# A third buffer for the samples' caches, and the attention sink as a 257th score column

## The reference, cut to what matters

```
def sink_attention(q, k, v, mask, sink):
    s = einsum(q, k) * HEAD_DIM ** -0.5            # a block of 128 queries against 256 keys
    s = where(mask, s, -inf)
    m = maximum(max(s, axis=-1), sk)               # sk: the sink of the head
    p = exp(s - m)
    p = p / (sum(p, axis=-1) + exp(sk - m))
    return einsum(p, v)
```

```
q = (h @ w_xq_l).reshape(B, L, X_HEADS, X_HEAD_DIM)
s = einsum(q, mk) * X_HEAD_DIM ** -0.5
p = softmax(s); o = einsum(p, mv)
return o @ w_xo_l
```

## Time and profile before

| | before |
|---|---|
| median of 3 runs | 3469.14 us (3467.0 to 3477.67) |
| the profiled execution | 3462.95 us |
| its span, first to last instruction | 3461.2 us |
| mean granted TensorE clock | 0.98 of full speed |
| PE / PEld busy | 3247.4 us (94%) / 3077.2 us (89%) |
| DVE busy | 2324.1 us (67%) |
| ACT busy | 1185.9 us (34%) |
| POOL busy | 679.0 us (20%) |
| DMA | 245.87 MB, mean 71 GB/s |

### The profile page before, as it was taken

The page is one execution under the profiler, slowest core; times in us unless marked ns, Lnnn a source line. Parts: engine busy times, 40 slices in busy tenths (PEclk is TensorE's granted clock), DMA queues, the critical chain, the costliest instruction groups (busy, mean ns, idle before and its releaser), DMA issues. The chain is left out here.

```text
span 3461.2 us, 51914 instructions
## 1 busy us (share of the span) xinstructions
PE 3247.4 (94%) x21872; PEld 3077.2 (89%) x21872; DVE 2324.1 (67%) x3509; ACT 1185.9 (34%) x1849; POOL 679.0 (20%) x274
## 2 busy tenths in 40 slices
PE   7999889899899999999989998898998999999997
PEld 7998769788799999999889987698887999999996
DVE  6776782834467677777787767737345767777776
ACT  5342363434432222212344424533344222222212
POOL 1111131012312212222111111310123221212220
PEclk9999999999899999999999999999999999999998
DMA  5112223213411111111121122332044111111111
GB/s 177 44 44 63 76 80 128 75 43 119 183 50 43 49 43 55 39 54 43 54 82 40 50 68 73 107 111 73 26 158 157 43 50 43 49 43 55 40 57 52
DMA packets 71176, 245.87 MB, mean 71 GB/s; under 512 B 7969, under 2 KB 22561, under 8 KB 65825
## 3 DMA queue, kind: packets, MB, share of 16 engines
q1 hardware_dynamic: 70656, 242.50, 20.7%
q10 hardware_dynamic: 288, 0.06, 0.0%
HBM read 214.20 MB, written 23.04 MB: 69 GB/s over the span
## 5 line engine op out<-in xcount | busy, mean ns | idle before, releaser
L258 PE MATMUL ps<-hh,w_hi 128*128 128x344 f32 (+2 forms) x4320 | 1417.6, 328 | 84.1 <-DVE w_lo L252 26.0
L260 PE MATMUL ps<-hh,w_lo 128*128 128x344 f32 (+2 forms) x4320 | 1391.2, 322 | 0.0
L259 PE MATMUL ps<-hl,w_hi 128*128 128x344 f32 (+2 forms) x4320 | 1391.0, 322 | 0.0
L243 POOL TENSOR_TENSOR w_lo<-w_raw,w_hi 128x1024 fp32r<-128x1024 f32 x270 | 678.8, 2516 | 2719.6 <-ACT w_hi L235 2719.6
L258 PEld LDWEIGHTS ps<-hh,w_hi 128*128 128x128 f32 x4320 | 822.8, 190 | 112.8 <-issue 53.5
L259 PEld LDWEIGHTS ps<-hl,w_hi 128*128 128x128 f32 x4320 | 822.0, 190 | 3.2 <-issue 1.1
L260 PEld LDWEIGHTS ps<-hh,w_lo 128*128 128x128 f32 x4320 | 822.0, 190 | 0.0
L2591 DVE TENSOR_TENSOR Y<-Y,ps 128x344 f32<-128x344 f32 x912 | 433.2, 513 | 155.7 <-PE ps L260 155.7
L235 ACT ACTIVATE w_hi<-w_raw 128x1024 fp32r<-128x1024 f32 x296 | 310.6, 1052 | 440.6 <-PE ps L260 383.8
L2390 ACT ACTIVATE f_c<-f_u,cT 128x1032 f32<-128x1032 f32 (+1 forms) x92 | 111.4, 1213 | 634.6 <-DVE f_u L2556 628.0
L259 PE MATMUL ps<-f_glo,w_hi 128*128 128x344 f32 x960 | 308.0, 321 | 0.0
(11 more groups left out here) (356 smaller groups left out, 3730.0 us busy)
## 6 DMA issues: line engine op xcount, KB each, us to landing
w_raw<-in_w_stream SPq DMA_DIRECT2D x296, 512.0 KB, 3.5
out_y_cols<-xT SPq DMA_DIRECT2D x9, 1376.0 KB, 6.3
xT<-out_y_cols SPq DMA_DIRECT2D x2, 4128.0 KB, 14.0
mem_keys<-in_cache_mem_k SPq DMA_DIRECT2D x8, 1024.0 KB, 5.0
mem_values<-in_cache_mem_k SPq DMA_DIRECT2D x8, 1024.0 KB, 6.3
mem_keys<-in_cache_mem_v SPq DMA_DIRECT2D x8, 1024.0 KB, 5.1
mem_values<-in_cache_mem_v SPq DMA_DIRECT2D x8, 1024.0 KB, 6.9
xT<-in_x_cols SPq DMA_DIRECT2D x3, 1376.0 KB, 12.4
```

Of the source, the lines that this page charges most:

```text
L243: nc.gpsimd.tensor_tensor(w_lo[:, SLOT[m], :], w_raw[:, m % RR, :], w_hi[:, SLOT[m], :].bitcast(F32), ALU.subtract).then_inc(lo_done["pool ...
L258: nc.tensor.matmul(out, whi, mhi, start=start, stop=False)
L259: nc.tensor.matmul(out, whi, mlo, start=False, stop=False)
L260: return nc.tensor.matmul(out, wlo, mhi, start=False, stop=stop)
```

## The change

Two edits that share nothing.

**The caches** get three buffers in turn: the keys' tile, columns 768 to 1023 of the 8 slices of `Y` (8 pieces of 1 KB on each partition), and the values' tile. Transfers 0 and 1 wait for the prompt's last scores, transfer 2 for its last values, transfer t from 3 on for the sample t - 3. In PE's order, one sample moves ahead of each of unit(1, 6) and unit(1, 7).

```
-                    return flat[t % 2]
+                    tiles = (mkT[:], Y[:, :, 768:SEQ], mv_tile[:])
+                    return tiles[t % 3]
...
                     def caches(t):
-                        if t >= 2:
-                            sp.wait_ge(s["s_done"], t - 1)
-                        elif t == 1:
+                        if t >= 3:
+                            sp.wait_ge(s["s_done"], t - 2)
+                        elif t == 2:
                             sp.wait_ge(s["pv"], 32)
                         else:
                             sp.wait_ge(s["scores"], n)
...
                     caches(0)
                     caches(1)
+                    caches(2)
                     load_slabs(sp, first + 2)
-                    for t in range(2, 2 * NS):
+                    for t in range(3, 2 * NS):
                         caches(t)
                         if t in (4, 6, 8):
                             load_slabs(sp, first + t // 2 + 1)
...
-                    sample_values(8)
-                    sample_values(9)
+                    for t in (8, 9, 10):
+                        sample_values(t)
                     unit(1, 6)
-                    sample_values(10)
                     sample_values(11)
+                    sample_values(12)
                     mean(1)
                     unit(1, 7)
-                    for t in (12, 13, 14, 15):
+                    for t in (13, 14, 15):
                         sample_values(t)
```

```
+                SK = 2 * P + 1
+                S = [xT[:, i, 0:4 * SK] for i in (5, 6, 7)]
...
                             for h in range(4):
-                                act_c(nc.scalar.activation(view(S[g % 3], g)[:, h, :], view(S[g % 3], g)[:, h, :], ACT.Exp,
-                                                           bias=st[:, 1, h:h + 1], accum_out=st[:, 3, h:h + 1]))
-                            nc.scalar.activation(st[:, 4, :], st[:, 2, :], ACT.Exp).then_inc(s["exp"], 1)
+                                last = nc.scalar.activation(view(g)[:, h, :], view(g)[:, h, :], ACT.Exp,
+                                                            bias=st[:, 1, h:h + 1], accum_out=st[:, 2, h:h + 1])
+                            last.then_inc(s["exp"], 1)
+                            if g + 3 < n:
+                                act.wait_ge(s["exp"], g + 1)
+                                sink_column(g + 3)
+
+                        def sink_column(g):
+                            sk = sinks[:, l, :].rearrange("p (k a j) -> p a k j", k=NKV, a=2)[:, g % 2]
+                            nc.scalar.activation(sink_view(g), sk, ACT.Copy).then_inc(s["sinks_in"], 1)
...
                             dve.wait_ge(s["scores_used"], g + 1)
+                            dve.wait_ge(s["sinks_in"], g + 1)
...
-                            dve_c(nc.vector.tensor_reduce(st[:, 0, :], sv, AX.X, ALU.max))
-                            dve_c(nc.vector.tensor_tensor(top, top, sk, ALU.max))
-                            dve_c(nc.vector.tensor_tensor(diff, sk, top, ALU.subtract))
+                            dve_c(nc.vector.tensor_reduce(st[:, 0, :], view(g), AX.X, ALU.max))
                             nc.vector.tensor_scalar(st[:, 1, :], st[:, 0, :], -1.0, None, ALU.mult).then_inc(s["negmax"], 1)
...
-                            dve_c(nc.vector.tensor_tensor(st[:, 3, :], st[:, 3, :], st[:, 4, :], ALU.add))
-                            dve_c(nc.vector.reciprocal(st[:, 5, :], st[:, 3, :]))
+                            dve_c(nc.vector.reciprocal(st[:, 3, :], st[:, 2, :]))
```

More of the change, by code:

```diff
@@ L391, in stage_window @@
                 vtok = rs[:, 0:SEQ].rearrange("p (b d) -> p b d", b=NB)
-                S = [xT[:, i, 0:1024] for i in (5, 6, 7)]
+                SK = 2 * P + 1
+                S = [xT[:, i, 0:4 * SK] for i in (5, 6, 7)]
                 PT = [xT[:, i, 0:1024] for i in (0, 1)]
-                small = tmp("win_small", [P, 3, 8, 4])
+                small = tmp("win_small", [P, 3, 4, 4])
                 mh, ml = tmp("mem_hi", [P, KT, NMEM], F32R), tmp("mem_lo", [P, KT, NMEM], F32R)
@@ L397, in stage_window @@
                 s = {n: sem(f"w_{n}") for n in (
-                    "v_turned", "v_copied", "kv_out", "scores", "scores_used", "negmax", "exp", "probs", "turned",
+                    "v_turned", "v_copied", "kv_out", "sinks_in", "scores", "scores_used", "negmax", "exp", "probs", "turned",
                     "turned_copied", "pv", "out_hi", "out_used", "rows_hi", "rows_lo", "mem_in", "m_hi", "m_lo", "m_out", "t_done",
@@ L407, in keys_of, with view, keys_view, sink_view @@
                     return P if g < 2 else 0
-                def view(t, g):
-                    return t.rearrange("p (h k) -> p h k", h=4)[:, :, keys_of(g):]
+                def view(g):
+                    return S[g % 3].rearrange("p (h k) -> p h k", h=4)[:, :, keys_of(g):]
+                def keys_view(g):
+                    return S[g % 3].rearrange("p (h k) -> p h k", h=4)[:, :, keys_of(g):2 * P]
+                def sink_view(g):
+                    return S[g % 3].rearrange("p (k j c) -> p k j c", k=NKV, j=2)[:, :, :, 2 * P]
                 def scores_of(g):
@@ L461, in turn @@
                                     last = nc.tensor.transpose(ps[:, 4 + half, P * h:P * h + P],
-                                                               S[g % 3][:, 256 * h + P * half:256 * h + P * half + P], ident[:])
+                                                               S[g % 3][:, SK * h + P * half:SK * h + P * half + P], ident[:])
                             last.then_inc(s["turned"], 1)
@@ L542, in copy @@
                                                  ps[:, 4 + h0:6, :], ACT.Copy).then_inc(s["turned_copied"], 1)
+                        for g in range(3):
+                            sink_column(g)
                         act.wait_ge(s["v_turned"], 1)
@@ L597, in before @@
                             dve.wait_ge(s["scores_used"], g + 1)
+                            dve.wait_ge(s["sinks_in"], g + 1)
                             st = small[:, g % 3]
-                            sk = sinks[:, l, :].rearrange("p (k a j) -> p a k j", k=NKV, a=2)[:, g % 2]
-                            top, diff = (st[:, i, :].rearrange("p (k j) -> p k j", k=NKV) for i in (0, 2))
-                            dve_c(nc.vector.tensor_reduce(st[:, 0, :], sv, AX.X, ALU.max))
-                            dve_c(nc.vector.tensor_tensor(top, top, sk, ALU.max))
-                            dve_c(nc.vector.tensor_tensor(diff, sk, top, ALU.subtract))
+                            dve_c(nc.vector.tensor_reduce(st[:, 0, :], view(g), AX.X, ALU.max))
                             nc.vector.tensor_scalar(st[:, 1, :], st[:, 0, :], -1.0, None, ALU.mult).then_inc(s["negmax"], 1)
@@ L1770, in stage_cross_ffn @@
                     "sq", "acc_used", "sqp", "out", "mean", "root", "rt_used", "x", "hh", "hl")}
-                kv_in = [sem(f"xs_in{i}") for i in range(2)]
+                kv_in = [sem(f"xs_in{i}") for i in range(3)]
                 scale = 256 ** -0.5
@@ L2030, in caches @@
                         which, b = divmod(t, NS)
-                        sp.dma_start(cache(t), io[("cache_mem_k", "cache_mem_v")[which]][l, b]).then_inc(kv_in[t % 2], 16)
+                        rows8 = io[("cache_mem_k", "cache_mem_v")[which]][l, b].rearrange("p (k c) -> p k c", k=KT)
+                        sp.dma_start(cache(t), rows8).then_inc(kv_in[t % 3], 16)
                     clear(sp, "ws", "oq")
@@ L2143, in sample_scores @@
                             pe.wait_ge(s["q_ready"], 1)
-                        pe.wait_ge(kv_in[t % 2], 16 * (t // 2 + 1))
-                        keys = cache(t).rearrange("p (k t) -> p k t", k=KT)
+                        pe.wait_ge(kv_in[t % 3], 16 * (t // 3 + 1))
+                        keys = cache(t)
                         for d in range(2):
@@ L2163, in sample_values @@
                             pe.wait_ge(s["out_lo"], 32)
-                        pe.wait_ge(kv_in[t % 2], 16 * (t // 2 + 1))
-                        v = cache(t).rearrange("p (a f) -> p a f", a=2)
+                        pe.wait_ge(kv_in[t % 3], 16 * (t // 3 + 1))
+                        v = cache(t)
                         for a in range(2):
```

9 lines of the change are left out of this document (4 added, 5 removed).

## The result

| | before | after |
|---|---|---|
| median, on one chip | 3470.01 us (3467.0 to 3477.67, 4 runs) | 3419.02 us (3414.89 to 3425.52, 4 runs) |
| ratio | | 0.9851, 95% interval [0.9827, 0.9876] |
| the profiled execution | 3462.95 us | 3425.52 us, span 3423.7 |

The change takes 51.0 us off the median. The two profiled executions differ by 37.5 us only: before's took 4 us less than the fastest of its four runs, and after's is the slowest of its four. So what follows goes by stretches of work and not by the ends of the spans.

The account below looks back on a forecast made before the run. TensorE, busy 94% of the span, was taken as the bound, so only its waits or slow clock could be won: 29.8 us (third buffer) + 11 (sink column) = 41 us, from the 3469.14 us median to 3428, range 3413 to 3447.

Parts of the forecast that it names:

- Third buffer: Sample sections: three caches at hand, transfers' rate sets the pace; 13.5 + 14.1 us, with 2.2 us of clock 29.8 us.
- just free: Softmax between samples 7 and 8: DVE and ACT finish the residual's work by 868.0, before sample 7 ends at 869.
- The load into Y: Cache loads in 1 KB pieces: 3.0 us of the queues taken per cache, 9.2 us as the other end.
- rates over 350 GB/s: Sign to show: queue rates over 350 GB/s through most of the sample section, itself about 51 us in both layers.
- Rival 2: Sample sections: queues don't hold full rate with mixed transfers, 324 GB/s; the gain there 15 us, 3443 us; chance 0.17.
- The clock of the third chunk's first unit: After layer 0's last samples: with shorter waits this unit runs at clock 1.00, giving 2.2 us back.
- Sink column: Window sections: three small DVE instructions gone per group; 0.4 us for each of 28 groups, 11 us.
- The forecast for the turn's wait: Window sections: PE's wait for DVE's last multiplication about 15 us in all and not 26.5.
- 1 (the loop through POOL's lock carries the section, 0 to 4 us): Window section: removed instructions lie under the loop through POOL's lock, gaining 0 to 4 us; 3437 us; chance 0.20.
- 3 (pieces of 1 KB): Loads into Y take 9.2 us and not 2.76, adding 26 us per layer; 3481 us; chance 0.04.
- 4 (later waits take the gain): PE finds later waits of the same size, on the third chunk's weights; 3460 to 3469 us; chance 0.04.
- The 257-column rows: Rows of S 257 columns apart: the gap between rows costs DVE nothing that could be seen.

Follow-up runs that it names:

- experiment 2: Order of the four exponentials: the sink column alone with them chained, 0.9943 of before; the kernel before with them unchained, 1.0002 of before.
- experiment 3: Changed kernel with ACT's high half of a slab ahead of the copy of turned probabilities: 3401.80 us; the same with the sink's old instructions: 3424.34 us.

## Why the prediction was right, point by point

The time, 3419.02 us, lies in the range and 9 us under the forecast. The sum had 29.8 + 11 = 41 us; measured alone the terms are 27.5 and 21.5. The forecast holds by its larger term. The smaller one is half of what was measured, and this leaves the sum 10 us short of the 51, which the range takes in.

**Third buffer: right in mechanism and size.** The chain of transfers gave sections of about 51 us; they took 52.7 and 51.8. The samples' softmax, which the prediction found "just free", held PE up by 0.8 and 0.6 us, and the caches' waits came to 8.3 us where under 8 were to show. The load into Y was taken at 3.0 us of the queues. Cache 1, issued 0.4 us behind cache 0, lands 7.9 us later, and cache 0 alone takes 5.0; that is 3.3 us between the two landings in layer 0; in layer 1 it is 4.0, and in the other kernels 2.9 to 4.4. Two caches in whole rows, issued 0.86 us apart in before (848.68 and 849.54), land 2.5 us apart. The issue is dearer for SP too (the row gives min/median/max in ns):

```profile
L2047 SPq DMA_DIRECT2D mem_keys<-in_cache_mem_k x6: 327/328/328, 798.7 to 2546.9; - x6
L2047 SPq DMA_DIRECT2D Y<-in_cache_mem_k x6: 551/589/653, 799.1 to 2552.3; - x6
```

Three windows of after hold full rates. Two don't, because the queues run empty for a part of them: the cache of sample 11 goes out when sample 8 is done, 8.2 us after the slab ahead of it. SP's timeline, then the windows:

```profile
862.30 0.34 SPq L226 DMA_DIRECT2D w_raw<-in_w_stream  x1
870.50 0.33 SPq L2047 DMA_DIRECT2D mem_values<-in_cache_mem_v  x1
```

```profile
846.00:854.00 8.00, 8.00 (x67) 6.51 (x66) 7.93 (x4) 2.07 (x4) 6.05 (x2) 1.00 1.00 398
854.00:862.00 8.00, 6.94 (x61) 5.46 (x60) 5.30 (x5) 7.97 (x16) 4.21 (x2) 1.00 1.01 382
862.00:870.00 8.00, 7.24 (x50) 6.46 (x52) 7.06 (x15) 3.35 (x8) 0.27 (x1) 1.00 0.72 264
870.00:878.00 8.00, 7.15 (x77) 5.60 (x72) 5.23 (x6) 4.19 (x9) 2.39 (x1) 1.00 0.78 261
878.00:886.00 8.00, 6.53 (x54) 4.97 (x45) 2.55 (x1) 1.46 (x2) 0.00 (x0) 1.00 1.05 405
```

So rates over 350 GB/s "through most of it" held for three windows of these five; over the whole sections the mean is 326 and 330. Rival 2 (the queues don't hold 380) fell: with work queued they moved 382 to 405 GB/s, and a stretch of before that the prediction did not look at, 887.5 to 895.5, already had 412. That is more than the 358 GB/s which the Trainium skill (DMA: Bandwidth & Descriptors, "Where 436 GB/s comes from") has as what binds a load from HBM. It gets this figure by sharing a stack's 716 GB/s between two cores, and this kernel runs on one; no run here shows what a second core would do to it.

**The clock of the third chunk's first unit: missed.** 2.2 us were given to layer 0, and a clock of 1.00 was to show. It did show there, but the two layers together gained 1.0 us. From the first sample to the end of that unit, less the section, layer 0 went from 7.3 to 4.9 us, but layer 1 from 4.9 to 6.3, since there the unit began at the lower level. The stretches are layer 1's unit, then layer 0's:

```profile
2592.20:2595.30 3.10, 3.10 (x14) 3.10 (x15) 0.00 (x0) 0.00 (x0) 0.00 (x0) 0.50 0.02 5
892.00:894.90 2.90, 2.90 (x25) 2.90 (x26) 0.00 (x0) 0.00 (x0) 0.00 (x0) 1.00 0.00 0
```

The waits ahead of the two units are the same within 0.1 us (1.1 for the last cache, 0.5, 0.8); why the clock differs, the trace does not show.

**Sink column: right in sign, half in size.** The term that was mis-sized is "Over such a pair I find 0.9 us. I take 0.4 us for each of 28 groups": 11 us, where the column alone measured 21.5. At 487 I saw the multiplication overtake POOL and then gave the gain away again: "the next large instruction is held in its place". It is held (L652, 3.42 us), but no turn waits for it. An overtaken lock is worth 1.6 to 1.7 us in the time between two turns, and it happened in three groups of layer 0 (turn to turn, us: 6.75 to 5.18, 7.65 to 6.01, 6.71 to 4.98). Five groups won 0.54 to 0.67 us each (8.15 to 7.57, say), which is the stream's own 0.6; four won less than 0.2 (6.73 to 6.72, say); the other three won 0.94, 0.39 and 0.48. It is a wide spread under one mean. The forecast for the turn's wait, about 15 us of 26.5, held (13.1). What the sum left out besides is 6.9 us that are not the turn's wait. They are PE's busy time, which fell by 2.5 us in layer 0 and 4.5 in layer 1. The granted clock, 0.97 and 0.95 before and 0.98 in both layers after, gives about 1 and 3 us of it; for the rest I have no cause.

**Rivals.** 1 (the loop through POOL's lock carries the section, 0 to 4 us) fell as stated, but its loop was real: with the split ahead of the copy another 17 us come out, and held multiplications fall from four or more to one in a layer. 3 (pieces of 1 KB) fell with three buffers: 2.9 to 4.4 us for a load are far from the 9.2 that it took and from the 8 from which it decides. With two buffers its mechanism shows, at some 7 us. 4 (later waits take the gain) fell: sections and medians agree, 47.0 us in the sections with the unit behind the samples (26.7 + 20.3) and 51 us by the medians.

**What was costed at nothing.** The 257-column rows: the maximum over 1028 elements takes 1.22 us like 1024 before, and the multiplication out of such rows has the median of 1225 ns that it had. DVE's wait for the sink's column never shows in layer 0's window. ACT's exponentials without their order bring nothing (experiment 2).

## What to carry to other kernels

Where one engine's long instruction locks another out, time removed ahead of it has no price of its own: here it was worth next to nothing, or its own 0.6 us, or, when it let an instruction get in first, 1.6 to 1.7 us, most of the stall; and the stall may only move to the next small instruction, as experiment 3 without the column shows. So list for each repetition which of the two starts first and by how much, before multiplying by a count, and see whether the lock's start hangs on the locked instruction; here one line moved in ACT's list cut that tie and gave 17 us.

In this ring the number of transfers under way paid; starting the second one earlier had nothing to give, since nobody had waited for it. Look for that wait first. And a new buffer is free only if what makes it free comes before its turn on the issuing queue, since everything behind waits too.

## What the runs showed that I had not expected

- A wait of PE can cost more than its length. In the sample sections of before, 26.0 us of idle time went with a clock of 0.92 and 0.90; with 9.7 us idle it was 1.00, and the same matmuls took 9.4 us less. Two buffers with longer waits gave 0.87 and 0.88. It is not a fixed price: layer 0 of the kernel before with its exponentials unchained had 13.0 us idle at a clock of 0.97, where before had 13.8 at 0.92.
- A DVE instruction that gets in first delays POOL by as much: POOL's splits at 412.63, 481.63 and 495.19 took 3.05 to 3.28 us and not 2.4, and a small one of 4 elements stands still too when POOL is first (2.29 us).
- A load of 1 MB in pieces of 1 KB lands 2.9 to 4.4 us behind the one ahead of it, where one in whole rows lands 2.5 us behind, and SP takes 0.55 to 0.65 us to issue one, for 0.33 us.
